# A quarter of the output projection between the transposes of the probabilities and those of the meta tokens

## Chip, cores and metric

The kernel runs on one core of one Trainium2 chip. Its time is the device time of one launch in microseconds (us); where several launches are told, it is their median. The engines of the core are named as in the profile: PE is TensorE (PEld is its row of weight loads), DVE is VectorE, ACT is ScalarE, POOL is GpSimd, and SP issues the DMA transfers of this part of the kernel.

## What is computed

The reference is a decoder trunk of two layers over 16 meta tokens and 2048 tokens of width 1024. Layer 0 is a gated delta rule with its projections; then one shared K/V is made; layer 1 is attention in a sliding window of 128 over blocks of 128 queries, in which the 16 meta tokens are visible to every query, followed by a gate, an output projection, the residual and a final RMSNorm. The change touches layer 1 alone:

```python
def sink_attention(q, k, v, mask, sinks):
    logits = jnp.einsum("bnqhgd,bnkhd->bnhgqk", q, k) * (SWA_HEAD_DIM ** -0.5)
    logits = jnp.where(mask[None, :, None, None], logits, NEG_BIG)
    m = jnp.maximum(jnp.max(logits, axis=-1, keepdims=True), s)   # s: a sink for each head
    p = jnp.exp(logits - m)
    den = jnp.sum(p, axis=-1, keepdims=True) + jnp.exp(s - m)
    return jnp.einsum("bnhgqk,bnkhd->bnqhgd", p / den, v)
...
    # swa_sink_mixer: keys of a block are [16 meta, 128 of the block before, 128 of its own]
    o_real = sink_attention(qr, band(k), band(v), mask, sinks_g)
    o = o * jax.nn.silu(z)
    return o @ w_out
```

There are 16 query heads of width 64 on 4 key/value heads.

## The kernel before

The program has four stages, one after the other. The fourth, `attention`, is written out engine by engine with semaphores by hand: each engine has a function `step(t, s, now, nxt, last)`, and `run` calls it for t = -1 to 16. No scheduler changes the order; each engine does its instructions in the order in which the code issues them and stops at a wait whose semaphore has not come. One step t works on three blocks of 128 queries at once: it does the attention of block t (`now`), the query projection of block t + 1 and a part of that of t + 2 (`nxt`), and the output projection of block t - 1 (`last`). Steps 2 to 13 are a hardware loop of two steps in a turn; step 0 has no output projection, and step 15 has no query projection.

What PE does in a step, in its order:

- `band_logits(t, s, u)` for u = 0 to 3 (line L2397), with pieces of the query projection between them (L2366, into `first_q`), and `meta_logits` (L2378), the logits of the meta tokens, into the bank `p4_psm`; then the rest of the query projection of block t + 1.
- `output_projection(t - 1, start, end)` (L2366 into `p_pso`): 48 matmuls of 512 columns, numbered 0 to 47. Of these `half` is 24, `early` is 12, so half of `early` is 6: a quarter of the second half. Matmuls 0 to 23 fill the first bank, 24 to 47 the second.
- `turn(t, g)` for g = 0 to 3 (L2441): each transposes four heads' probabilities into a bank of `p_psr`. DVE masks them on their way to SBUF (`transposed`, L2264, two copies a group: of the block before and of the own one).
- `turn_meta(t)` (L2430): two transposes of `p_pm`, in which DVE has packed the probabilities of the meta tokens of all 16 heads (L2245, the end of `normalise`), into `p_psm`. ACT copies the result to `p_pmT` (L2149).
- `values(t, s, g)` for g = 0 to 3: for g = 0 and 2 first four matmuls with `p_pmT` (L2456), then for each g four with the masked probabilities and v (L2465, of a stationary tile of 128 x 64, where the others have 128 x 128).
- `query_transposes(t + 1)` (L2477).

In the trace a matmul of fp32 operands (L2397, L2456, L2465, L2378) has two records, a transpose or one of the projections has one. DVE's order in a step is: merging and masking of the logits (L2214 to L2217), maxima (L2230), the query bias, `normalise` for eight heads at a time (L2240 to L2245), the masked copies of groups 0 and 1, the residual's first half, group 2, the gate, and so on. DVE signals `band_ready` after the masked merge, for which PE waits ahead of the last two groups of band logits. The wait on which `turn_meta` stands is `pm_ready`, which DVE's second packing signals:

```python
def turn_meta(t):
    pe.wait_ge(pm_ready, 2 * (t + 1))
    pe.wait_ge(meta_ready, t + 1)
...
def values(t, s, g):
    b = g // 2
    if g % 2 == 0:
        if g == 0:
            pe.wait_ge(pmT_ready, t + 1)
```

Of the kernel before, what the change touches and what calls it, by code (L numbers as in the profile page):

```python
# [1907 lines left out]
def attention(nc, wo_d, b_q, sinks, final, rope, consts, wq, ps_q, h1_d, hT_d, gate_d, kT_d, v_d, out_d, raw):  # L1908
# [6 lines left out]
    with nc.cleanup_on_exit(), ExitStack() as ctx:  # L1915
# [108 lines left out]
        def is_first(t):  # L2024
            return isinstance(t, int) and t == 0
# [331 lines left out]
        def _(pe):  # L2357
# [14 lines left out]
            def meta_logits(t):  # L2372
                if is_first(t):
                    pe.wait_ge(meta_in, 16 * N_META_IN)
                else:
                    pe.wait_ge(pmT_ready, t)
                for c in range(QH // 2):
                    last_ = nc.tensor.matmul(ps_m[:, c * 2 * META:(c + 1) * 2 * META], qT[:, c, :], km[:, c // 4, :],  # L2378
                                             start=True, stop=True)
                last_.then_inc(meta_ps, 1)  # L2380

            def band_logits(t, s, u):

                if u == 0:
                    pe.wait_ge(qT_ready, 2 * (t + 1))
                    pe.wait_ge(k_in[s], 16 * ((t + (2 - s)) // 2))
                    if not is_first(t):
                        pe.wait_ge(pT_ready, 4 * t)
                if u >= 2:
                    pe.wait_ge(band_ready, 8 * t + (2 * u - 2))  # L2390
                for c in (2 * u, 2 * u + 1):
                    for x, slot in ((0, 1 - s), (1, s)):
                        for i in range(2):
                            if x or not is_first(t):
                                rows = slice(i * HD, (i + 1) * HD)
                                col = (2 * (c % 2) + x) * P
                                last_ = nc.tensor.matmul(pairs[u % 2][i][:, col:col + P], qT[rows, c, :],  # L2397
                                                         kT[rows, slot, c // 4, :], start=True, stop=True)
                                if x and c % 2:
                                    last_.then_inc(band_ps, 1)  # L2400

            def query_projection(t, start, end):
                def before(b, kc):
                    if b == 0 and kc == 0:
                        pe.wait_ge(hT_in, 32 * t)
                    if kc == 0 and isinstance(t, int) and t == 1:
                        pe.wait_ge(q_read, 1 + b)
                    if kc == 0 and not (isinstance(t, int) and t < 2):
                        pe.wait_ge(weighed, 2 * t - (3 - b))

                product(ps_q, hT, wq, start, end, q_ps, before)
# [13 lines left out]
# [4 lines that stand above are left out]
                for b in range(2):  # L2429
                    last_ = nc.tensor.transpose(ps_m[:, b * P:(b + 1) * P], pm[:, b * P:(b + 1) * P], ident[:])  # L2430
                last_.then_inc(pmT_ps, 1)

            def turn(t, g):

                pe.wait_ge(normalised, 2 * t + (g // 2 + 1))
                if g < 3:
                    pe.wait_ge(band_ready, 8 * (t + 1))
                else:
                    pe.wait_ge(pT_ready, 4 * t + (g - 2))
                for n in range(4):  # L2440
                    last_ = nc.tensor.transpose(ring[(2 + g) % 3][:, n * P:(n + 1) * P], logits[:, 4 * g + n, 0:P],  # L2441
                                                ident[:])
                last_.then_inc(pT_ps, 1)
# [8 lines that stand above are left out]
                        if not (isinstance(t, int) and t == NT - 1):  # L2452
                            pe.wait_ge(q_read, 2 * (t + 2))
                        pe.wait_ge(v_in[s], 16 * ((t + (2 - s)) // 2))
                    for r in range(4):
                        nc.tensor.matmul(ps_q[b][:, r * P:(r + 1) * P], vm[:, b, 2 * r * HD:(2 * r + 2) * HD],  # L2456
                                         pmT[:, b, :], start=r == 0, stop=False)
                pe.wait_ge(pT_ready, 4 * t + (g + 1))
                cols = slice(2 * (g % 2) * P, (2 * (g % 2) + 2) * P)
                for x, slot in ((0, 1 - s), (1, s)):  # L2460
                    if x or not is_first(t):
                        for i in range(2):
                            kvh = 2 * b + i
                            moving = pT[:, g % 2, x, :].rearrange("p (r i k) -> p r i k", r=2, i=2)[:, :, i, :]
                            last_ = nc.tensor.matmul(ps_q[b][i * HD:(i + 1) * HD, cols].rearrange("p (r k) -> p r k", r=2),  # L2465
                                                     v[:, slot, kvh * HD:(kvh + 1) * HD], moving, start=False,
                                                     stop=g % 2 == 1 and x == 1)
                last_.then_inc(pv_ps, 1)

            def query_transposes(t):  # L2470
                if is_first(t):
                    pe.wait_ge(const_in, 16 * N_CONST)
                pe.wait_ge(q_turned, 2 * (t + 1))
                if not (isinstance(t, int) and t < 2):
                    pe.wait_ge(h_ready, 2 * (t - 1))
                for kc in range(KC):
                    last_ = nc.tensor.transpose(ps_o[kc // 4][:, kc % 4 * P:(kc % 4 + 1) * P],  # L2477
                                                q[:, kc // 4, kc % 4 * P:(kc % 4 + 1) * P], ident[:])
                last_.then_inc(qT_ps, 1)

            def step(t, s, now, nxt, last):
                half = 3 * KC
                early = half // 2
                if isinstance(t, int) and t == -1:
                    query_projection(1, 0, early)
                    query_transposes(0)
                    return
                for u in range(4):
                    if now:
                        band_logits(t, s, u)  # L2490
                    if nxt:
                        query_projection(t + 1, early + u * early // 4, early + (u + 1) * early // 4)
                    if now and u == 0:
                        meta_logits(t)
                if nxt:
                    query_projection(t + 1, half, half + early // 2)
                if nxt:
                    query_projection(t + 1, half + early // 2, 2 * half)
                if last:
                    output_projection(t - 1, 0, half)  # L2500
                if now:
                    turn(t, 0)
                    turn(t, 1)
                    turn_meta(t)
                if last:
                    output_projection(t - 1, half, half + early // 2)
                if now:
                    values(t, s, 0)
                if last:
                    output_projection(t - 1, half + early // 2, half + early)  # L2510
                if now:
                    turn(t, 2)
                    values(t, s, 1)
                if last:
                    output_projection(t - 1, half + early, 2 * half)
                ahead = nxt and not (isinstance(t, int) and t in (-1, NT - 2))
                if now:
                    turn(t, 3)
                if ahead:
                    query_projection(t + 2, 0, early // 3)  # L2520
                if now:
                    values(t, s, 2)
                if ahead:
                    query_projection(t + 2, early // 3, 2 * early // 3)
                if nxt:
                    query_transposes(t + 1)
                if ahead:
                    query_projection(t + 2, 2 * early // 3, early)
                if now:
                    values(t, s, 3)  # L2530

            run(pe, step)


# [122 lines left out]
```

## Time and profile before

| | before |
|---|---|
| time, median of 3 launches | 2793.78 us (2791.85 to 2794.45) |
| time of the profiled launch | 2792.86 us |
| its span, first to last instruction | 2790.9 us |
| PE busy | 2501.1 us, 90% |
| DVE busy | 1675.1 us, 60% |
| ACT busy | 1137.0 us, 41% |
| granted clock of PE, mean | 0.957 |
| length of one step of the fourth stage's loop | 39.2 us |

Some 1.96 us of the profiled launch lie outside the span. PE's busy time is an average over the four stages; of the fourth stage only its own steps tell what a change there is worth. A granted clock of 1.00 is 2.4 GHz, one of 0.50 is 1.2 GHz.

### The profile page before, as it was taken

How to read it: one execution, taken by the hardware profiler on the slowest of the kernel's cores; microseconds unless marked ns; L12 is line 12 of the kernel's file. 1: busy time of each engine (PE TensorE's matmuls, PEld its weight loads, DVE VectorE, ACT ScalarE, POOL GpSimd, SP SyncE). 2: the span in 40 equal slices, each digit the busy share in tenths (PEclk: the TensorE clock that was granted, in tenths of full speed). 3: DMA queues.
4: the chain of work that ended last, by engine and by line, in shares of the span. 5: the costliest groups of instructions: out<-in, count | busy, mean ns of one | idle time of the engine just before them, and what ended most of it. 6: DMA issues, size and time to landing. Idle time of an engine off the chain costs nothing. (4 is left out here: it accounts for less than half of the span.)

```text
span 2790.9 us, 50427 instructions
## 1 busy us (share of the span) xinstructions
PE 2501.1 (90%) x17193; PEld 2195.6 (79%) x17193; DVE 1675.1 (60%) x3904; ACT 1137.0 (41%) x3326; POOL 456.7 (16%) x345
## 2 busy tenths in 40 slices
PE   5568888899999999999999689999997999999997
PEld 4467777789998999999999568878885777777775
DVE  4367676677777777777777333333332667666664
ACT  4244454544444444444444244433332233333332
POOL 0133343210000000000000012100001333323331
PEclk8689999999999999999999689999997999999998
DMA  6664354544445444444353067643455222222221
GB/s 190 204 246 143 138 170 148 176 133 132 141 139 186 140 146 124 133 151 136 120 171 97 22 205 254 243 157 140 180 199 232 68 69 85 85 69 75 68 69 48
DMA packets 273814, 392.79 MB, mean 141 GB/s; under 512 B 79282, under 2 KB 187906, under 8 KB 273442
## 3 DMA queue, kind: packets, MB, share of 16 engines
q1 hardware_dynamic: 240066, 370.05, 39.9%
q10 hardware_dynamic: 33632, 21.26, 2.6%
q8 instruction: 65, 1.06, 0.2%
q14 instruction: 51, 0.42, 0.0%
HBM read 267.92 MB, written 123.31 MB: 140 GB/s over the span
## 5 line engine op out<-in xcount | busy, mean ns | idle before, releaser
L1229 PE MATMUL p_psp<-xg,p_whi 128*128 128x264 f32 x4096 | 846.0, 296 | 26.2 <-POOL p_wlo L1178 17.2
L1229 PEld LDWEIGHTS p_psp<-xg,p_whi 128*128 128x128 f32 x4096 | 658.2, 192 | 30.8 <-issue 21.5
L1229 PE MATMUL p_psp<-xg,p_wlo 128*128 128x264 f32 x2048 | 608.2, 297 | 0.0
L1229 PEld LDWEIGHTS p_psp<-xg,p_wlo 128*128 128x128 f32 x2048 | 392.9, 192 | 0.0
L981 DVE SCALAR_TENSOR_TENSOR p_acc<-p_proj,p_taps,p_acc 128x528 f32<-128x528 f32 x288 | 250.8, 871 | 4.6
L1824 PE MATMUL first_q<-first_w,p_o 128*128 128x512 f32 (+1 forms) x864 | 206.5, 398 | 16.3 <-DVE first_w L1788 16.3
L2366 PE MATMUL first_q<-first_w,p_hT 128*128 128x512 f32 x720 | 196.8, 413 | 13.9 <-DVE p_q L2252 13.5
L1824 PEld LDWEIGHTS first_q<-first_w,p_o 128*128 128x128 f32 (+1 forms) x864 | 156.8, 184 | 59.2 <-issue 14.2
L2366 PE MATMUL p_pso<-p_wo,p_oT 128*128 128x512 f32 x768 | 194.4, 404 | 7.9 <-DVE p_oT L2278 4.2
L862 ACT ACTIVATE p_sig<-p_sig 128x528 f32<-128x528 f32 x128 | 82.7, 646 | 291.5 <-DVE p_sig L983 291.4
L2366 PEld LDWEIGHTS p_pso<-p_wo,p_oT 128*128 128x128 f32 x768 | 143.7, 192 | 48.7 <-issue 16.1
L1824 PE MATMUL p_psz<-p_wk,p_o 128*128 128x512 f32 x768 | 181.2, 392 | 0.0
L1023 DVE TENSOR_TENSOR p_prod<-p_Xb,p_blk 32x4 f32<-32x4 f32 (+13 forms) x448 | 165.4, 369 | 6.8
L2366 PEld LDWEIGHTS first_q<-first_w,p_hT 128*128 128x128 f32 x720 | 129.9, 192 | 49.5 <-issue 20.6
L1824 PEld LDWEIGHTS p_psz<-p_wk,p_o 128*128 128x128 f32 x768 | 142.9, 188 | 29.1
L1178 POOL TENSOR_TENSOR p_wlo<-raw,p_whi 128x512 fp32r<-128x512 f32 x72 | 106.3, 1487 | 273.4 <-ACT p_whi L843 273.2
L2123 ACT ACTIVATE p_logits<-p_logits,p_top 128x144 f32<-128x144 f32 x256 | 103.3, 405 | 86.1 <-DVE p_top L2233 86.1
L1189 POOL TENSOR_TENSOR p_kg<-p_kT,p_er 128x512 f32<-128x512 f32 (+1 forms) x40 | 44.8, 1125 | 553.6 <-ACT p_er L879 553.5
L2346 POOL TENSOR_TENSOR p_swapped<-p_q,p_cs 128x256 f32<-128x256 f32 x32 | 37.3, 1167 | 594.4 <-DVE p_q L2252 592.1
L854 ACT ACTIVATE p_proj<-p_psp 128x264 f32<-128x264 f32 x256 | 99.5, 389 | 62.6 <-PE p_psp L1229 61.5
L1194 POOL TENSOR_TENSOR p_qd<-p_qT,p_er 128x512 f32<-128x512 f32 (+1 forms) x40 | 51.3, 1291 | 436.3 <-DVE p_qT L1003 436.3
L1025 DVE TENSOR_REDUCE p_Xb<-p_prod 32x2 f32<-32x4 f32 (+13 forms) x448 | 104.9, 234 | 15.4
(263 smaller groups left out, 4655.9 us busy)
## 6 DMA issues: line engine op xcount, KB each, us to landing
p_whi<-w_dram SPq DMA_DIRECT2D x92, 512.0 KB, 4.1
p_wlo<-w_dram SPq DMA_DIRECT2D x92, 512.0 KB, 4.8
raw<-w_a_in SPq DMA_DIRECT2D x36, 512.0 KB, 6.3
w_dram<-p_whi SPq DMA_DIRECT2D x34, 512.0 KB, 4.1
w_dram<-p_wlo SPq DMA_DIRECT2D x34, 512.0 KB, 5.2
p_o<-hT_dram SPq DMA_DIRECT2D x34, 512.0 KB, 4.9
hT_dram<-p_hT SPq DMA_DIRECT2D x32, 512.0 KB, 3.4
p_hT<-hT_dram SPq DMA_DIRECT2D x30, 512.0 KB, 4.1
```

Source lines behind the costliest of these rows:

```text
L854: nc.scalar.activation(proj[:, f % 2, 3 + half_ * HALF:3 + (half_ + 1) * HALF], ps_p[half_][:, 0:HALF], ACT.Copy).then_inc(proj_read, 1)
L862: ins = nc.scalar.activation(v, v, ACT.Exp, scale=-1.0)
L981: nc.vector.scalar_tensor_tensor(a, p[:, part:part + GW], w, a, ALU.mult, ALU.add).then_inc(tap_done, 1)
L1023: link(nc.vector.tensor_tensor(t3, x3[:, 0:i, 0:i].rearrange("p j c -> p c j"), b3[:, 0:i, i].unsqueeze(1).to_broadcast([rows, i, i]), ALU ...
L1025: link(nc.vector.tensor_reduce(x3[:, i, 0:i], t3, mybir.AxisListType.X, ALU.add))
L1178: nc.gpsimd.tensor_tensor(w_lo[:, f, cols], w_raw[:, f % 2, cols], w_hi[:, f, cols].bitcast(f32), ALU.subtract).then_inc(lo_ready, 1)
L1189: nc.gpsimd.tensor_tensor(kg[p.par][:, at, :], cols(kT), e_r[:, at, :], ALU.mult).then_inc(keys_grown, 1)
L1194: nc.gpsimd.tensor_tensor(qd[p.par][:, at, :], cols(qT), e_r[:, at, :], ALU.mult).then_inc(queries_grown, 1)
L1229: ins = nc.tensor.matmul(ps_p[half_][:, 0:HALF], (w_hi, w_lo)[i][:, f, kc * P:(kc + 1) * P], xg[:, g % 2, j, kc, half_ * HALF:(half_ + 1) ...
L1824: last = nc.tensor.matmul(out, stationary[i][:, kc, 0:rows], moving(j, kc), start=kc == 0 and n == 0, stop=kc == KC - 1 and n == 2)
L2123: last_ = nc.scalar.activation(logits[:, s_, :], logits[:, s_, :], ACT.Exp, bias=top[:, s_:s_ + 1], accum_out=den[:, s_:s_ + 1])
L2366: ins = nc.tensor.matmul(banks[b][:], stationary[i][:, kc, :], weights[j][:, kc, b * FB:(b + 1) * FB], start=kc == 0 and n == 0, stop=kc = ...
```

## The change

In `step` of PE, two calls change places with pieces of the output projection. `turn_meta(t)` moves behind matmuls 24 to 29 of the output projection, and `values(t, s, 0)` moves behind matmuls 30 to 35. No instruction is added or removed, and no wait of any function is changed. The code of the other engines is as it was.

```diff
                 if now:
                     turn(t, 0)
                     turn(t, 1)
-                    turn_meta(t)
                 if last:
                     output_projection(t - 1, half, half + early // 2)
                 if now:
-                    values(t, s, 0)
+                    turn_meta(t)
                 if last:
                     output_projection(t - 1, half + early // 2, half + early)
                 if now:
+                    values(t, s, 0)
                     turn(t, 2)
                     values(t, s, 1)
                 if last:
```

On PE, in step 1 (and alike in each step from 1 to 15), between the first half of the output projection and the second group of values; `p_psr` takes the transposed probabilities, `p_psm` those of the meta tokens, `first_q` the values, `p_pso` the output projection:

```order
 L2366 MATMUL p_pso<-p_wo,p_oT 128x512 x24
 L2441 MATMUL p_psr<-p_ident,p_logits 128x128 x8
+L2366 MATMUL p_pso<-p_wo,p_oT 128x512 x6
 L2430 MATMUL p_psm<-p_ident,p_pm 128x128 x2
 L2366 MATMUL p_pso<-p_wo,p_oT 128x512 x6
 L2456 MATMUL first_q<-p_pmT,p_vm 128x128 x4
 L2465 MATMUL first_q<-p_pT,p_v 64x256 x4
-L2366 MATMUL p_pso<-p_wo,p_oT 128x512 x6
 L2441 MATMUL p_psr<-p_ident,p_logits 128x128 x4
 L2465 MATMUL first_q<-p_pT,p_v 64x256 x4
```

Six matmuls that stood between the first values and the third group of transposes now stand ahead of the transposes of `p_pm`. The third group of transposes now stands between two groups of values with nothing else beside it.

On PE in step 0, before and after the change the same, since there is no output projection yet:

```order
2571 L2441 MATMUL p_psr<-p_ident,p_logits 128x128 x8
2572 L2430 MATMUL p_psm<-p_ident,p_pm 128x128 x2
2573 L2456 MATMUL first_q<-p_pmT,p_vm 128x128 x4
2574 L2465 MATMUL first_q<-p_pT,p_v 64x256 x2
2575 L2441 MATMUL p_psr<-p_ident,p_logits 128x128 x4
2576 L2465 MATMUL first_q<-p_pT,p_v 64x256 x2
```

Nothing moved here; it is the one place of the kernel before in which transposes of `p_logits` stand directly between two groups of values.

## Rows read from the trace of the kernel before

**Rows 1.** The page's first line.

```profile
span 2790.9 us, 50427 instructions
```

**Rows 2.** Windows: length; busy us of PE, PEld, DVE, ACT, POOL; clock; DMA.

```profile
2429.60:2468.80 39.20, 38.40 (x252) 30.12 (x251) 25.41 (x47) 13.25 (x48) 12.41 (x9) 1.00 0.22 75
...
2703.80:2739.00 35.20, 32.25 (x227) 25.64 (x225) 24.77 (x44) 12.75 (x47) 12.40 (x9) 1.00 0.21 68
2739.00:2770.00 31.00, 23.69 (x118) 18.18 (x119) 19.26 (x35) 11.05 (x42) 2.35 (x1) 0.86 0.07 23
```

**Rows 3.** Timeline of one step: start, us, engine, line, operation, idle before.

```profile
2440.51 1.03 PE L2441 MATMUL p_psr<-p_ident,p_logits 128*128 128x128 f32 x8
2441.66 0.63 DVE L2245 COPY p_pm<-p_logits 128x128 f32<-128x128 f32 x1
...
2442.34 0.44 PE L2430 MATMUL p_psm<-p_ident,p_pm 128*128 128x128 f32 x2 [0.80 <-DVE p_pm L2245]
...
2442.54 1.64 PE L2366 MATMUL p_pso<-p_wo,p_oT 128*128 128x512 f32 x6
...
2442.82 0.39 ACT L2149 ACTIVATE p_pmT<-p_psm 128x256 f32<-128x256 f32 x1 [5.00 <-PE p_psm L2430]
...
2444.01 0.67 DVE L2264 TENSOR_TENSOR p_pT<-p_psr,p_own_T 128x512 f32<-128x512 f32 x1
2444.01 1.05 PE L2456 MATMUL first_q<-p_pmT,p_vm 128*128 128x128 f32 x8
...
2444.99 1.08 PE L2465 MATMUL first_q<-p_pT,p_v 128*64 128x256 f32 x8
2446.01 1.23 PEld L2366 LDWEIGHTS p_pso<-p_wo,p_oT 128*128 128x128 f32 x6 [0.38 <-issue]
...
2447.50 0.60 PE L2441 MATMUL p_psr<-p_ident,p_logits 128*128 128x128 f32 x4
2448.03 0.63 PEld L2465 LDWEIGHTS first_q<-p_pT,p_v 128*64 128x64 f32 x8 [0.17 <-issue]
...
2449.05 3.03 PE L2366 MATMUL p_pso<-p_wo,p_oT 128*128 128x512 f32 x12
```

**Rows 4.** Who waited for the tile p_pm, fourth stage: us, times.

```profile
  PEld p_psm L2430: 14.2, 14
  PE p_psm L2430: 10.8, 14
```

**Rows 5.** Timeline of PE in steps 14 and 15.

```profile
2714.71 1.03 PE L2441 MATMUL p_psr<-p_ident,p_logits 128*128 128x128 f32 x8
2716.30 0.44 PE L2430 MATMUL p_psm<-p_ident,p_pm 128*128 128x128 f32 x2 [0.56 <-DVE p_pm L2245]
...
2750.42 1.03 PE L2441 MATMUL p_psr<-p_ident,p_logits 128*128 128x128 f32 x8
2751.29 0.38 PE L2430 MATMUL p_psm<-p_ident,p_pm 128*128 128x128 f32 x2
```

**Rows 6.** Waits in steps 1 to 13: us in total, times, longest.

```profile
PEld p_pso L2397 <- DVE p_logits L2217: 0.4, 1, 0.4
```

**Rows 7.** Timeline of weight loads between groups of values, steps 0 and 14.

```profile
2176.15 0.72 PEld L2441 LDWEIGHTS p_psr<-p_ident,p_logits 128*128 128x128 f32 x4 [0.76 <-issue]
...
2177.20 0.30 PEld L2465 LDWEIGHTS first_q<-p_pT,p_v 128*64 128x64 f32 x4 [0.33 <-issue]
...
2728.30 0.86 PEld L2477 LDWEIGHTS p_pso<-p_ident,p_q 128*128 128x128 f32 x8 [0.39 <-issue]
2729.32 0.63 PEld L2465 LDWEIGHTS first_q<-p_pT,p_v 128*64 128x64 f32 x8 [0.17 <-issue]
```

**Rows 8.** Timeline of PE: output projections in steps 9, 15 and 16.

```profile
2474.23 5.61 PE L2366 MATMUL p_pso<-p_wo,p_oT 128*128 128x512 f32 x24
...
2742.14 8.44 PE L2366 MATMUL p_pso<-p_wo,p_oT 128*128 128x512 f32 x24 [3.75 <-DVE p_logits L2217]
...
2768.33 12.74 PE L2366 MATMUL p_pso<-p_wo,p_oT 128*128 128x512 f32 x48 [4.17 <-DVE p_oT L2278]
```

## The prediction

> **What bounds the kernel now.** I read the page's first line for the span, then the windows of single steps of the fourth stage, then one step instruction by instruction, then the waits around the tile that the moved transposes read. The span is 2790.9 us [rows 1]; the profiled launch took 2792.86 us, 0.92 us less than the median of 2793.78 us. A step in the middle of the loop lasts 39.2 us, and PE is busy for 38.40 of them, at a granted clock of 1.00, which is 2.4 GHz; DVE is busy for 25.41, ACT for 13.25, POOL for 12.41, and the DMA engines for 0.22 of the time [rows 2]. So a step is as long as PE's list of instructions and PE's waits. The idle time left over is 39.20 - 38.40 = 0.80 us, and the timeline has a wait of just that size: ahead of the two transposes of the meta tokens' probabilities, 0.80 us, ended by DVE's packing of `p_pm` [rows 3]. The reader is to see that this packing starts at 2441.66 and takes 0.63, so it ends at 2442.29, and the first transpose starts at 2442.34.
>
> The same wait comes in 14 steps: 10.8 us on PE's row of matmuls and 14.2 us on its row of weight loads [rows 4]. The two differ because the end of a matmul in the trace is modelled. I measure by starts instead. In the middle step the eight transposes of groups 0 and 1 start at 2440.51 and the meta transposes at 2442.34, 1.83 us later [rows 3]. In step 15, where nothing is waited for, the same distance is 2751.29 - 2750.42 = 0.87 [rows 5]. The wait is worth 1.83 - 0.87 = **0.96 us**. In step 14 the distance is 2716.30 - 2714.71 = 1.59 [rows 5], and in step 1 it is the same, so these two wait 0.72 us each. Steps 0 and 15 gain nothing: the first has no output projection to put in, the last has no wait.
>
> **The change part by part.** Nothing is added or removed; I follow PE through the middle step with the starts of [rows 3].
>
> 1. Six matmuls of the output projection go ahead of the meta transposes. They start where these could have started, at 2440.51 + 0.87 = 2441.38. Six of them, up to the start of transposes that follow, take 2447.50 - 2446.01 = 1.49 us. So PE comes to the meta transposes at 2442.87, and `p_pm` has been there since 2442.29. The wait is gone, with 0.58 us to spare. If that cover were missing, PE would wait again for what is missing and no more.
> 2. The meta transposes and the next six matmuls cost what they did: 0.20 (2442.34 to 2442.54) and 1.47 (2442.54 to 2444.01). The first matmul with `p_pmT` starts at 2442.87 + 0.20 + 1.47 = 2444.54. ACT must have copied `p_pmT` by then: it started 0.48 us after the meta transposes began and took 0.39, thus 2442.87 + 0.48 + 0.39 = 2443.74. That is hidden, with 0.80 us to spare. ACT itself is idle there: it had stood for 5.00 us.
> 3. The values of group 0 follow: 0.98 us (2444.01 to 2444.99) and then L2465 at 2445.52. It needs group 0's masked copies. DVE's last copy of groups 0 and 1 ends at 2444.01 + 0.67 = 2444.68, which covers group 1's values too.
> 4. The third group of transposes now comes right behind, 1.02 us later (2444.99 to 2446.01 is the distance from such values to what follows), at 2446.54. Before it was 2447.50. **PE is 0.96 us ahead**, and from here on its order is that of before: values of group 1, twelve matmuls, and so on.
>
> What is late next? I looked for work that does not move with PE. DVE's masked copy of group 2 starts after the transposes; DVE has been idle between the residual's first half and it, so it moves along. The gate, the twelve matmuls, ACT's statistics, POOL's scaling, the store and the loads all start from something that PE has done, and the DMA engines are busy for 0.22 of a step. DVE's long chain from band logits to `p_pm` starts with PE's band logits and therefore comes earlier as well: the distance between PE's band logits and its arrival at the transposes of groups 0 and 1 isn't touched, so the 0.58 us of step 1 of this list stay the same in every step. The nearest other wait is that for DVE's merged logits ahead of the last band logits: one time in 13 steps, 0.4 us [rows 6]. Its two ends both lie behind the same band logits, so it stays as it is.
>
> One operation stands where it hardly stood before: transposes directly between two groups of values. A group of values has a stationary tile of 128 x 64, its neighbours have 128 x 128. In the order of before, PE's weight loads stand idle for 0.38 us behind the values and for 0.17 us ahead of them [rows 3]. In step 14, transposes of the queries stand directly between two groups of values at full clock, with 0.39 and 0.17 us [rows 7]. The number of such passages in a step is the same before and after, two into values and two out of them, so I take 0 for it. In step 0 the very sequence of the new order stands, with 0.76 and 0.33 us [rows 7], but there PE ran at half the clock, and the values are twice as short. As the worst end I take those two numbers as they are: (0.76 - 0.38) + (0.33 - 0.17) = 0.54 us a step. I choose 0 since the rows of step 14 have the clock of the loop.
>
> The Trainium skill has a rule on this place (TensorEngine Tiling (Array Packing), Key Properties): a change of the tiling mode, not just of the tile, drains TensorE. The 0.38 and 0.17 us at exactly these passages agree with it. By the rule a short group of transposes between two changes has less work of its own to hide them under; if it then costs as in the worst end, the sum is that of the first rival below.
>
> The sum: 12 steps at 0.96 are 11.5 us, 2 steps at 0.72 are 1.4 us, together **13.0 us**. The profiled launch of 2792.86 us would become 2779.9 us, and against the median 2793.78 - 13.0 = **2780.8 us**. The bounds of the wait itself are the two totals: 10.8 and 14.2 us [rows 4].
>
> One term can only be bounded. In step 15 PE stands for 3.75 us, and then 24 matmuls of the output projection take 8.44 us, where 24 take 5.61 us in the loop; the granted clock of that stretch is 0.86 on average, so it has been at 1.2 GHz for part of it [rows 2, 8]. The 48 matmuls of the end take 12.74 us after 4.17 us of idle time, 1.5 us more than twice 5.61 [rows 8]. When exactly the clock falls and returns is not tied to the program, as far as one launch shows, and the change moves both places. I take 0 for it and up to 8.44 - 5.61 = 2.8 us to either side.
>
> **The rivals.**
>
> *The passages between the shapes cost more.* The third group of transposes pays 0.54 us in each of 15 steps, 8.1 us in all. The time is 2793.78 - 13.0 + 8.1 = 2788.9 us. For it: step 0's rows. Against it: step 14's, and that doubled numbers are what half the clock would give. Chance 0.06.
>
> *The wait only moves.* PE arrives 0.96 us earlier in each step at everything, and some other wait takes that back: that for the merged logits, for instance, which already shows once [rows 6]. For it: with PE busy for 38.40 of 39.20 us any partner that is tied to a fixed rhythm would show at once. Against it: no partner with such a rhythm is to be found, DVE has some 14 us of idle time in a step, and the transfers are far from their limit. The time is 2793.8 us, no change. Chance 0.06. A small part of the wait could come back in the same way, which the range holds.
>
> *The clock falls inside the loop.* Between the second six matmuls and the twelve, PE now has values, transposes and values and no projection, some 3.5 us (0.98 + 1.02 + 0.5 + 1.02). If the clock fell to 1.2 GHz there, the price would be that of step 15, 2.8 us for such a stretch, in 14 steps 39.6 us, and the time 2793.78 - 13.0 + 39.6 = 2820 us, slower than before. It decides from 0.93 us a step on, a third of that price. Against it: the clock is 1.00 in the loop [rows 2], and 1.00 too in step 14, whose last third has no projection at all; it fell only after PE had stood still for 3.75 us [rows 8], and the change takes idle time away. Chance 0.04.
>
> **How the numbers follow.** The forecast has a chance of 0.84. Its own range is from 2793.78 - 14.2 - 2.8 = 2776.8 to 2793.78 - 10.8 + 2.8 = 2785.8 us. To hold 8 in 10 over all cases I carry it a little toward the first rival and give 2776.5 to 2787.0 us. A measurement of this kernel tells 0.2%, 5.6 us, from no change, so below 2788.2 us is faster. The forecast lies there wholly, and a half of the first rival and of the partial forms with it: faster 0.87, the same 0.09, slower 0.04.
>
> **What the changed profile would show.** The wait of PE for `p_pm` is gone from steps 1 to 14, and six matmuls of the output projection stand ahead of L2430. A step of the loop takes 38.2 us in place of 39.2, with PE's busy time still about 38.2 to 38.4. The distance from the first of the eight transposes to the first L2456 grows from 3.50 to 4.0 us, and that from L2465 of group 0 to L2465 of group 1 falls from 3.04 to about 1.6 us. The idle marks of the weight loads around the third group of transposes read 0.38 and 0.17. The granted clock stays at 1.00. The prediction is wrong if L2430 still waits (then `p_pm` came later against PE than in step 1 of the list), if L2456 now waits for ACT, if a new wait of about 1 us stands ahead of band logits, or if the marks around the third group are far above 0.4.

## The result, and the profile after

The kernel became faster by half a per cent: the median went from 2794.45 us (7 launches, 2791.85 to 2797.79) to 2779.97 us (7 launches, 2775.80 to 2787.00), and the ratio is 0.9946, with a 95% interval of 0.9936 to 0.9955. That is 14.5 us by the medians and 15.1 us by the ratio. The prediction had said 2780.8 us. The two times lie only 0.8 us apart partly by chance: the forecast of a fall of 13.0 us started from a median of 2793.78 us, and more launches of the kernel before have raised that to 2794.45.

The profiled launch of the changed kernel is its slowest: 2787.00 us, with a span of 2785.0 us. Its trace must be read by stretches, then. It came to the eight transposes of step 1 at 2216.16 us, where the launch of before came at 2205.68, although the program up to there is the same. From these transposes to those of step 14 it took 2710.76 - 2216.16 = 494.60 us, against 2714.71 - 2205.68 = 509.03 before: 14.43 us less in 13 steps. The rest up to the end took 1.95 us less. Together 10.48 - 14.43 - 1.95 = -5.9 us, which is the difference of the two spans.

The windows of the changed kernel, for one step from meta transposes to meta transposes (columns as in [rows 2]):

```profile
2446.69:2484.74 38.05, 38.05 (x251) 30.10 (x250) 25.39 (x47) 13.15 (x47) 12.44 (x10) 1.00 0.23 78
```

The step takes 38.05 us, and PE is busy for all of it; before it was 38.40 of 39.20 [rows 2]. So the step became shorter by more than the 0.80 us of idle time that it had: PE's busy time itself fell by 0.35 us, where the prediction had left it at 38.2 to 38.4. The eight transposes count as 1.03 us busy in both kernels, while the matmuls behind them now start 0.79 us after them; 0.24 us of the old wait had been counted as work. The clock is 1.00 still. The same step in the timeline, answering to [rows 3]:

```profile
2444.44 1.03 PE L2441 MATMUL p_psr<-p_ident,p_logits 128*128 128x128 f32 x8
...
2445.23 1.63 PE L2366 MATMUL p_pso<-p_wo,p_oT 128*128 128x512 f32 x6
2445.59 0.65 DVE L2245 COPY p_pm<-p_logits 128x128 f32<-128x128 f32 x1
...
2446.46 0.37 PEld L2430 LDWEIGHTS p_psm<-p_ident,p_pm 128*128 128x128 f32 x2
2446.69 0.38 PE L2430 MATMUL p_psm<-p_ident,p_pm 128*128 128x128 f32 x2
...
2446.83 1.62 PE L2366 MATMUL p_pso<-p_wo,p_oT 128*128 128x512 f32 x6
...
2447.11 0.38 ACT L2149 ACTIVATE p_pmT<-p_psm 128x256 f32<-128x256 f32 x1 [5.38 <-PE p_psm L2430]
...
2448.29 1.05 PE L2456 MATMUL first_q<-p_pmT,p_vm 128*128 128x128 f32 x8
...
2449.27 1.08 PE L2465 MATMUL first_q<-p_pT,p_v 128*64 128x256 f32 x8
2450.28 0.42 PEld L2441 LDWEIGHTS p_psr<-p_ident,p_logits 128*128 128x128 f32 x4 [0.39 <-issue]
2450.87 0.63 PEld L2465 LDWEIGHTS first_q<-p_pT,p_v 128*64 128x64 f32 x8 [0.17 <-issue]
...
2451.89 3.02 PE L2366 MATMUL p_pso<-p_wo,p_oT 128*128 128x512 f32 x12
```

No row of PE or PEld in this step names DVE or ACT as the one that it waited for. DVE's packing ends at 2445.59 + 0.65 = 2446.24, and 0.22 us later the weight load of the meta transposes begins. It begins 0.23 us ahead of its matmul, which it could not do in the kernel before, where both started at 2442.34:

```profile
2442.34 0.20 PEld L2430 LDWEIGHTS p_psm<-p_ident,p_pm 128*128 128x128 f32 x2 [1.04 <-DVE p_pm L2245]
```

From the first of the eight transposes to the twelve matmuls it is 7.45 us, against 2449.05 - 2440.51 = 8.54 before: 1.09 of the 1.12 us that a step became shorter.

Who waited for the tile `p_pm` in the changed kernel, answering to [rows 4]; only ACT is left, which waits for the transposes at no cost to PE:

```profile
its engine sat idle before it (us, times) until:
who waited for it (us, times):
  ACT p_pmT L2149: 80.6, 15
```

In step 15 and at the end the half clock shows again, as in [rows 8], 0.68 and 0.29 us cheaper in this launch:

```profile
2737.34 7.76 PE L2366 MATMUL p_pso<-p_wo,p_oT 128*128 128x512 f32 x24 [3.75 <-DVE p_logits L2217]
...
2762.78 12.45 PE L2366 MATMUL p_pso<-p_wo,p_oT 128*128 128x512 f32 x48 [4.17 <-DVE p_oT L2278]
```

### The profile page after: what moved, and what is told of

Its sections match the earlier page's. It is cut to its first block and busy times, and to the rows that moved or that the text cites. A ratio compares the mean times of both kernels' runs of the same rounds, so it can differ in the third digit from the quotient of the medians.

```text
span 2785.0 us, 50427 instructions
## 1 busy us (share of the span) xinstructions
PE 2502.1 (90%) x17193; PEld 2202.9 (79%) x17193; DVE 1675.2 (60%) x3904; ACT 1132.9 (41%) x3326; POOL 457.1 (16%) x345
## 3 DMA queue, kind: packets, MB, share of 16 engines
q8 instruction: 65, 1.06, 0.2%
```

## The experiments

The launches of one kernel lie some us apart, so the size of a step is read from the traces: the distance from the eight transposes of step 1 to those of step 14, divided by 13. The table has it beside the ratio to before; the sections tell each run.

| kernel | matmuls ahead of the meta transposes, behind them up to the values | a step, us | ratio to before, interval |
|---|---|---|---|
| before | 0, 6 | 39.16 | 1 |
| change | 6, 6 | 38.05 | 0.9946 (0.9936 to 0.9955) |
| change again | 6, 6 | 38.05 | 0.9952 (0.9936 to 0.9967) |
| meta transposes alone moved | 6, 0 | 39.04 | 1.0003 (0.9994 to 1.0013) |
| values alone moved | 0, 12 | 39.06 | 0.9995 (0.9983 to 1.0006) |
| before, packing twice | 0, 6 | 39.82 | 1.0045 (1.0025 to 1.0064) |
| change, packing twice | 6, 6 | 38.40 | 0.9960 (0.9946 to 0.9974) |
| cover of three | 3, 9 | 38.39 | 0.9961 (0.9950 to 0.9972) |
| cover of nine | 9, 3 | 38.24 | 0.9963 (0.9950 to 0.9976) |
| third group early | 6, 6 | 37.76 | 0.9923 (0.9908 to 0.9937) |
| both pairs of values joined | 6, 6 | 37.45 | 0.9918 (0.9903 to 0.9933) |

### The meta transposes alone

```diff
                 if last:
                     output_projection(t - 1, half, half + early // 2)
                 if now:
                     turn_meta(t)
+                    values(t, s, 0)
                 if last:
                     output_projection(t - 1, half + early // 2, half + early)
                 if now:
-                    values(t, s, 0)
                     turn(t, 2)
```

(The diffs of this part are against the changed kernel, unless told otherwise.)

> The first half of the change alone: the meta transposes stand behind the six matmuls 24 to 29, the values of group 0 stay right behind the meta transposes. Theory (the gain is DVE's packing, hidden under the six matmuls): PE no longer waits for the packing, but the copy of the transposed meta probabilities on ACT, 0.48 + 0.39 us after the start of the meta transposes, now stands open ahead of the values, some 0.7 us a step. A step of the loop takes about 38.8 us, against 39.17 before and 38.05 with the whole change; the time falls by about 5 us against before (ratio 0.998). Rival (the gain comes from the place of the values, not from the wait): 39.17 us a step, ratio 1.000. Rival (ACT's copy costs PE nothing): 38.05 us a step, ratio 0.995.

A step took 39.04 us and the ratio is 1.0003: nothing is left of the gain, where I had expected a third of it. PE of this run, with the idle marks:

```profile
2326.18 0.38 PEld L2430 LDWEIGHTS p_psm<-p_ident,p_pm 128*128 128x128 f32 x2
2326.41 0.38 PE L2430 MATMUL p_psm<-p_ident,p_pm 128*128 128x128 f32 x2
2326.83 0.38 ACT L2149 ACTIVATE p_pmT<-p_psm 128x256 f32<-128x256 f32 x1 [5.40 <-PE p_psm L2430]
2327.43 0.97 PEld L2456 LDWEIGHTS first_q<-p_pmT,p_vm 128*128 128x128 f32 x8 [0.88 <-issue]
2327.46 1.13 PE L2456 MATMUL first_q<-p_pmT,p_vm 128*128 128x128 f32 x8 [0.67 <-ACT p_pmT L2149]
2328.52 0.63 PEld L2465 LDWEIGHTS first_q<-p_pT,p_v 128*64 128x64 f32 x8
```

The wait for the packing is gone and the wait for ACT has come in its place. From the start of the meta transposes to that of the values it is 1.05 us, where they are followed by matmuls of the projection after 0.14, and the values themselves take 1.06 us instead of 0.98; their first weight load no longer starts ahead of its matmul. Together that is the 0.99 us a step that was lost against the whole change. ACT's copy explains only a part of it: it ends 0.80 us after the start of the meta transposes, and the weight load comes 0.22 us later, marked `issue`, which means that PE waited for nothing that the profile shows. In steps 1, 14 and 15, outside the hardware loop, the same weight load comes 0.04 to 0.05 us behind the copy, and the values start 0.86 us after the meta transposes:

```profile
2717.37 0.39 ACT L2149 ACTIVATE p_pmT<-p_psm 128x256 f32<-128x256 f32 x1 [5.59 <-PE p_psm L2430]
2717.80 0.97 PEld L2456 LDWEIGHTS first_q<-p_pmT,p_vm 128*128 128x128 f32 x8 [0.71 <-ACT p_pmT L2149]
```

What takes the other 0.2 us in the loop is not shown. So the rival that put the gain down to the place of the values fits the total by chance, but its wait is another one; the next run parts them. Both halves of the change are needed, one for the wait for DVE and one for the way over ACT.

### The values alone

```diff
                     turn(t, 1)
+                    turn_meta(t)
                 if last:
                     output_projection(t - 1, half, half + early // 2)
-                if now:
-                    turn_meta(t)
                 if last:
                     output_projection(t - 1, half + early // 2, half + early)
```

> The second half of the change alone: the meta transposes stay right behind groups 0 and 1, and twelve matmuls stand between them and the values of group 0, which are followed directly by the third group of transposes. Theory: the wait for the packing stays whole, so a step takes 39.1 to 39.2 us and the ratio to before is 1.000. Rival (the gain comes from matmuls that are no longer split around the third group): a step takes about 38.1 us, ratio 0.995, although L2430 still waits.

```profile
2366.95 1.03 PE L2441 MATMUL p_psr<-p_ident,p_logits 128*128 128x128 f32 x8
2368.78 0.44 PE L2430 MATMUL p_psm<-p_ident,p_pm 128*128 128x128 f32 x2 [0.80 <-DVE p_pm L2245]
2368.97 3.00 PE L2366 MATMUL p_pso<-p_wo,p_oT 128*128 128x512 f32 x12
```

The distance of 1.83 us and the mark of 0.80 are those of [rows 3], and a step takes 39.06 us. Joining the six matmuls with the next six and setting the third group between the values saves 0.1 us and no more. The rival is out.

### The packing twice, in both orders

```diff
                 dve.wait_ge(normalised, 2 * t + (b + 1))
+                if b == 1:
+                    link(nc.vector.tensor_copy(pm[:, b * P:(b + 1) * P].rearrange("p (h k) -> p h k", k=META),
+                                               logits[:, sl, P:LW]))
                 nc.vector.tensor_copy(pm[:, b * P:(b + 1) * P].rearrange("p (h k) -> p h k", k=META),
```

In these two kernels the lines behind the edit have numbers that are larger by 3.

> The order of before, and DVE packs the second half of the meta probabilities twice (one more copy of 0.65 us and the wait for it, about 0.7 us). Theory: the packing is what a step waits for, so each of 14 steps grows by the 0.7 us to 39.9 us; the time rises by about 10 us, ratio 1.0035. Rival (the wait is a symptom, PE is bound elsewhere): less than 3 us, ratio 1.001 or below.

> The order of the change, and DVE packs the second half of the meta probabilities twice, about 0.7 us later. It tells how much room the six matmuls leave. By the starts of PE's matmuls in the changed kernel the room is 0.45 us (2446.24 to 2446.69), by its weight loads 0.2 us: a step grows by 0.25 to 0.5 us, to 38.3 to 38.55 us, and L2430 waits again for the packing. By the prediction's room of 0.58 us it grows by 0.1 to 0.15 us. Against before the ratio is 0.9965 to 0.998. Rival (the room is larger and the doubled copy is hidden): 38.05 us a step.

In the order of before a step grew by 39.82 - 39.16 = 0.66 us, the length of the added copy. All of it reached the time; the ratio of 1.0045 is above what 14 such steps give (0.66 x 14 = 9.2 us, 1.0033), but its interval holds that too. In the order of the change it grew by 0.35 us. Of the added 0.69 us (the packing now ends 2.49 us after the start of the eight transposes, where it ended after 1.80) 0.34 are hidden: that is the room that the six matmuls leave. The rows of the second run:

```profile
2410.67 1.03 PE L2444 MATMUL p_psr<-p_ident,p_logits 128*128 128x128 f32 x8
...
2412.50 0.66 DVE L2248 COPY p_pm<-p_logits 128x128 f32<-128x128 f32 x1
2413.21 0.20 PEld L2433 LDWEIGHTS p_psm<-p_ident,p_pm 128*128 128x128 f32 x2 [0.55 <-DVE p_pm L2248]
2413.22 0.44 PE L2433 MATMUL p_psm<-p_ident,p_pm 128*128 128x128 f32 x2
```

PE's matmuls carry no mark here. Who looks only at PE's row sees no wait, while a step is 0.35 us longer. PEld's row has the mark, and the waiters of the tile in the same run say so in total:

```profile
  PEld p_psm L2433: 7.4, 14
  PE p_psm L2433: 0.6, 3
```

### How many matmuls stand ahead of the meta transposes

```diff
-                    output_projection(t - 1, half, half + early // 2)
+                    output_projection(t - 1, half, half + early // 4)
...
-                    output_projection(t - 1, half + early // 2, half + early)
+                    output_projection(t - 1, half + early // 4, half + early)
```

and the same with `3 * early // 4` for nine. With them the changed kernel ran again.

> The changed kernel once more, beside the next two on the same chip. If the gain is 14 waits and nothing of the launch, a step of the loop takes 38.05 us again and the ratio to before is 0.9945 to 0.995, however the stages ahead of the fourth vary.

> The order of the change, but only three matmuls of the output projection (24 to 26) stand ahead of the meta transposes and nine behind them. Theory: three matmuls cover about 0.7 us less of the wait than six. The packing ends some 1.8 us after the start of the eight transposes, and PE comes to the meta transposes after 1.6 us, so 0.2 to 0.35 us of the wait are left: a step takes 38.25 to 38.4 us, the ratio to before is 0.996 to 0.9965. Rival (any matmul ahead of the meta transposes is enough): 38.05 us.

> The order of the change, but nine matmuls (24 to 32) stand ahead of the meta transposes and three behind them. The packing has been there for 1 us then, and the other round trip is the one that may show: ACT's copy, after which the first value could start 1.05 us after the meta transposes in the run with the meta transposes moved alone. Three matmuls and the transposes themselves cover about 0.9 us of it. A step takes 38.15 to 38.35 us, a little more than the 38.05 of the change, ratio to before 0.9955 to 0.996. Rival (only the packing matters, so nine is as good as six): 38.05 us.

The repeat gave 494.60 us for its 13 steps, the same hundredth as the first launch, and the ratio 0.9952. Three matmuls gave 38.39 us a step, with a remaining wait of 7.3 us in 14 steps on PEld's row and 0.2 us in all on PE's. Nine gave 38.24 us: the packing is covered, and the way over ACT isn't quite. In the run with nine:

```profile
2397.93 0.38 PE L2430 MATMUL p_psm<-p_ident,p_pm 128*128 128x128 f32 x2
2398.35 0.38 ACT L2149 ACTIVATE p_pmT<-p_psm 128x256 f32<-128x256 f32 x1 [6.07 <-PE p_psm L2430]
2398.95 0.97 PEld L2456 LDWEIGHTS first_q<-p_pmT,p_vm 128*128 128x128 f32 x8 [0.38 <-issue]
2398.98 1.13 PE L2456 MATMUL first_q<-p_pmT,p_vm 128*128 128x128 f32 x8
```

Here too the weight load comes 0.22 us behind the copy with the mark `issue`. What PE's weight loads waited for ahead of L2456 in this run, over steps 1 to 15:

```profile
  issue: 4.5, 12
  ACT p_pmT L2149: 0.6, 3
```

That is 0.38 us in each of the twelve steps of the loop and 0.2 in each of the three outside it. Step 1, outside the loop, is 38.10 us long, only 0.06 us more than step 1 of the change. So most of what nine matmuls lose in the loop stands behind ACT's copy and is not the copy.

With 0, 3, 6 and 9 matmuls a step takes 39.16, 38.39, 38.05 and 38.24 us. Of these four places six is the best, between the two waits. By their ratios alone the last three could not be told apart.

### Fewer passages between the shapes

Third group early:

```diff
                     turn_meta(t)
+                    turn(t, 2)
                 if last:
                     output_projection(t - 1, half + early // 2, half + early)
                 if now:
                     values(t, s, 0)
-                    turn(t, 2)
                     values(t, s, 1)
```

Both pairs joined, on top of it:

```diff
                 if ahead:
                     query_projection(t + 2, 0, early // 3)
-                if now:
-                    values(t, s, 2)
...
                 if ahead:
                     query_projection(t + 2, 2 * early // 3, early)
                 if now:
+                    values(t, s, 2)
                     values(t, s, 3)
```

> The order of the change, and the third group of transposes moved up to stand right behind the meta transposes, so that the values of groups 0 and 1 stand together: two passages between the stationary shapes 128 x 128 and 128 x 64 less in a step. If each costs what its idle mark shows (0.38 and 0.17 us, a part of it hidden), a step takes about 37.75 us, 0.3 us less than with the change alone, and the ratio to before is 0.993. Rival (the passages cost PE's matmuls nothing, so that their number does not matter): 38.05 us. Rival (the values of group 1 now come too early for DVE's masked copy): a wait ahead of L2465 and more than 38.05 us.

> The order of the change with both pairs of values joined: the third group of transposes stands behind the meta transposes, as in the run before, and the values of group 2 are moved down to stand right ahead of those of group 3. That takes away two more passages between the stationary shapes. By the starts of the rows of the changed kernel the stretch from the fourth matmul group of the query projection to the band logits falls from 6.92 to 6.60 us, so a step takes about 37.45 us, against 37.76 with the first pair alone, and the ratio to before is about 0.989. Rival (the passages were not what made the first pair faster): 37.76 us. Rival (the values of groups 2 and 3 come too late for DVE's gate and the band logits wait): more than 37.76 us.

Both steps came out as expected: 37.76 and 37.45 us. The ratio of the second did not: 0.989 was expected, and 0.9918 (0.9903 to 0.9933) was measured. Its 1.71 us a step in 15 steps are 25.6 us, which is 0.991, so 0.989 had not followed from the step. Each pair that is joined takes away two passages and 0.3 us. The rows of the first of the two runs:

```profile
2360.73 1.05 PE L2456 MATMUL first_q<-p_pmT,p_vm 128*128 128x128 f32 x8
2361.71 1.95 PE L2465 MATMUL first_q<-p_pT,p_v 128*64 128x256 f32 x16
2363.59 3.02 PE L2366 MATMUL p_pso<-p_wo,p_oT 128*128 128x512 f32 x12
```

Two groups of values take 2363.59 - 2361.71 = 1.88 us together, where in the changed kernel they and the transposes between them take 2451.89 - 2449.27 = 2.62 us. The transposes cost 0.35 us in their new place (2358.90 to 2359.25), and the meta transposes ahead of them 0.22 instead of 0.14 us. The kernel with both pairs has the lowest median of the study: 2771.49 us (6 launches), ratio 0.9918. No matmul of PE waits for another engine between steps 1 and 13. In step 14 a wait is new: without the values of group 2 ahead of them, the transposes of the queries wait for DVE:

```profile
2708.46 1.07 PE L2477 MATMUL p_pso<-p_ident,p_q 128*128 128x128 f32 x8 [0.44 <-DVE raw L2286]
```

The values are also another kind of matmul than their neighbours (two records each, where a transpose or a matmul of a projection has one), and both passages went with each pair. Whether the stationary shape or the kind costs the time, these runs don't part.

One thing does not add up at first. The third group alone made 0.29 x 15 = 4.4 us by its steps, but the medians of the runs on the same chip are 2780.88 and 2773.13 us, 7.8 us apart. The traces of the two profiled launches, 8.4 us apart by their spans, show where that lies: 494.60 - 490.88 = 3.7 us in the 13 steps, and 2209.54 - 2205.39 = 4.15 us ahead of the eight transposes of step 1. Of the latter 3.27 us had arisen at the first matmul of the meta logits (2154.84 and 2151.57), up to which the two programs are the same. For these two launches most of the rest lies ahead of anything that the edit moved.

## Why the prediction was right

**What bounds the kernel.** Right. A step was PE's work and one wait. Lengthening the packing lengthened the step by just as much, and with the wait hidden PE is busy for the whole of it.

**Step 1, the cover.** The mechanism was right, two sizes were not. The wait was put at 1.83 - 0.87 = 0.96 us; measured as what a step lost, it was 39.17 - 38.05 = 1.12 us, and in step 14 0.85 instead of 0.72 us. One error lies in taking 0.87 from transposes followed by transposes. Followed by projection matmuls they take 0.79. Another is what an uncovered start costs after the wait: from the meta transposes to the next matmuls it was 0.20 us and is 0.14. Step 15 of the kernel before shows how much of the 1.12 us was the wait, since it has the old order without one, at full clock:

```profile
2757.93 3.02 PE L2366 MATMUL p_pso<-p_wo,p_oT 128*128 128x512 f32 x12
```

From its eight transposes to these twelve matmuls it is 2757.93 - 2750.42 = 7.51 us. The same stretch took 8.54 in the middle step and takes 7.45 in the new order. So the wait was worth 1.03 us, which is the mark of 1.04 on the weight loads, and 0.06 us a step are the order alone; 0.03 us lie elsewhere in the step. The total over steps 1 to 14 is 14.43 + 0.85 = 15.3 us, not 13.0, which lies above the upper bound of 14.2 that I took from PEld's row. The room was given as 0.58 us; doubling the packing measured 0.34. The difference is again made of small terms. PE comes to the meta transposes 2.25 us behind the eight transposes and not 2.36, the packing ends after 1.80 and not 1.78, a matmul that waited starts some 0.05 us behind the packing, and the uncovered start costs 0.06: 0.58 - 0.11 - 0.02 - 0.05 - 0.06 = 0.34. The lead of 0.23 us that the weight load has over its matmul took nothing from the room. In the doubled run both begin together, at 2413.21 and 2413.22: the weight load comes 0.52 us later in its step than with the single packing and the matmul 0.30 us, and the step grew by 0.35.

**Step 2, ACT's copy.** It was hidden, as said: it ends at 2447.11 + 0.38 = 2447.49, 0.80 us ahead of the first matmul that reads it, which is the spare time forecast. That matmul starts 3.85 us behind the eight transposes and not 4.0, for the reasons of step 1. How much the cover is worth was shown by the run without the second six matmuls, in which the open way over ACT took back 1.0 of the 1.12 us. I had expected 0.7 there. In step 14, outside the loop, it cost 0.8 (8.25 - 7.45 us for the stretch used above); the remaining 0.2 us come only in the loop, and no row says for what.

**Steps 3 and 4, the order behind.** The third group came 1.15 us earlier against the eight transposes (6.99 us behind them before, 5.84 now), where 0.96 was forecast, and the rest moved along; no new wait appeared between steps 1 and 14. The passages around the transposes were taken as 0. Their marks read 0.39 and 0.17 us, where [rows 3] has 0.38 and 0.17, and the four transposes took 0.59 us in place of 0.53, so it cost 0.06 us. The change keeps the number of passages, which is why 0 was right; that they cost nothing would have been wrong, as the joined pairs show with 0.15 us each, of shape and kind together. The rule on them of the Trainium skill (TensorEngine Tiling (Array Packing), Key Properties), that a change of the tiling mode drains TensorE, is compatible with those 0.15 us. That these passages are changes of the mode no trace shows: it has the stationary shape alone. The first rival, that the short transposes pay 0.54 us more, does not come true with 0.06.

**The half clock** of step 15 moved within the bounds given to it. The 24 matmuls after the idle time of 3.75 us took 7.20 to 8.62 us in the eleven profiled launches of this study, against 8.44 in the one that the prediction had; none of the eleven was without it. That this part is a matter of the launch and not of the change is argued from the spread, not shown.

**The rivals.** The wait did not move elsewhere, and the clock stayed at 1.00 in the loop.

By the ratio the time fell by 15.1 us, 2.1 us more than forecast. The steps account for it: their 15.3 us against 13.0. For the launches alone 2 us would be too little to tell, since the interval reaches from 12.6 to 17.9 us.

## What to carry to other kernels

Where one engine bounds a loop and waits once for a short chain on another engine, its own independent work fits in that place; but count both waits, the one for the other engine and the one for what comes back: hiding the first without the second gave 0.12 us of 1.12. Measure a wait by the starts on both sides and in the row of the weight loads: in the doubled run a matmul without a mark stood behind 0.55 us of idle weight loads, and the step was 0.35 us longer. Once the waits are gone, the order still matters: each pair of groups of values that was put together saved 0.3 us a step, a quarter of what the change had been worth.

## What the hardware showed that I had not expected

This wait of TensorE cost more than its mark on the matmuls. It was 0.80 us by that mark, 1.04 by the mark of the weight loads, and 1.03 by the starts, against the same order without a wait. A wait that is partly covered is another matter: with a mark of 0.55 us on the weight loads the step was 0.35 us longer.

In the hardware loop the weight load that waits for ACT's copy starts 0.20 to 0.25 us behind it, outside the loop 0.04 to 0.05 us. This holds in both runs in which that wait is open, those with six matmuls ahead and none behind and with nine ahead.

The loop repeated from launch to launch (494.60 us for 13 steps in both profiled launches of the change), while what stands ahead of it did not. In the two profiled launches of before and of the change, the same program came to step 1 with 10.5 us between them. 7.7 us of that had arisen before the fourth stage began: DVE's clearing of `p_vm` started at 2122.22 and 2129.91. Another 2.5 us came from one small transfer into `p_vm`, which is the last of twenty that ACT issues one after the other: it took 17.80 us in the one launch and 20.32 in the other. The chain that ended last, of before and then of the changed kernel:

```profile
2133.26 17.80 DMA p_vm<-v_dram
```

```profile
2140.95 20.32 DMA p_vm<-v_dram
```

That part of the launches' difference says nothing of the change, and PE's first meta logits stand behind this transfer in both. It is a transfer of 4 KB; the two loads of `p_wo`, of 4 MB each, were under way at the same time and took some 20 us too. Whether it stands behind them was not tried.
